# The end of a hybrid trunk step rebuilt: the last expert's activations, down products and scatters

## The reference

```python
h2 = rms_norm(x, g_ffn) * (1.0 + sc_f) + sh_f
# for each expert e and each of its tokens:
hu = xe @ w_up[e] + b_up[e]
gate = jnp.minimum(hu[:, :D_FF], 7.0)
lin = jnp.clip(hu[:, D_FF:], -7.0, 7.0)
y = ((lin + 1.0) * gate * sigmoid(1.702 * gate)) @ w_down[e] + b_down[e]
# out[token] = sum over its 4 experts of softmax weight * y
x = x + gt_f * out
y_prompt, y_sample = rms_norm(x_prompt, g_final), rms_norm(x_sample, g_final)
```

## Time and profile before

| what | value |
|---|---|
| median of 3 runs | 1298.41 us (1296.67 to 1298.94) |
| the profiled execution's own time | 1295.37 us |
| its span, first to last instruction | 1293.6 us |
| TensorE matmul busy | 1163.6 us (90%) |
| TensorE weight loads busy | 567.3 us (44%) |
| DVE, ACT, POOL busy | 375.8, 182.7, 72.0 us |
| moved by DMA | 467.36 MB, mean 361 GB/s |
| mean granted TensorE clock | 0.970 of full speed |

### The profile page before, as it was taken

One profiled execution on the slowest core, in us unless ns is written; L12 is line 12 of the kernel. 1 busy time (PEld: TensorE's weight loads), 2 busy tenths in 40 slices (PEclk: granted clock), 3 DMA queues, 4 the chain that ended last, 5 costly groups with the idle time before them and its releaser, 6 DMA issues.

```text
span 1293.6 us, 23349 instructions
## 1 busy us (share of the span) xinstructions
PE 1163.6 (90%) x8690; PEld 567.3 (44%) x8691; DVE 375.8 (29%) x819; ACT 182.7 (14%) x358; POOL 72.0 (6%) x178
## 2 busy tenths in 40 slices
PE   5999999996989999998999998999777889988986
PEld 4655447544335446443344544444223334343332
DVE  0164214848211222321222121142211221222235
ACT  3112232213010111110110110010100000110101
POOL 1010001431000000000000000000000000000001
PEclk9999999998899999998999999999879999989999
DMA  9944635883689999999999999999999999999992
GB/s 366 363 152 172 239 131 196 253 317 138 260 351 424 409 417 427 427 428 425 428 424 426 426 426 428 426 376 428 427 426 428 426 425 426 426 426 428 427 422 85
DMA packets 62481, 467.36 MB, mean 361 GB/s; under 512 B 6538, under 2 KB 24910, under 8 KB 26730
## 3 DMA queue, kind: packets, MB, share of 16 engines
q1 hardware_dynamic: 59770, 461.86, 86.7%
q10 hardware_dynamic: 2288, 4.37, 1.1%
q0 software_dynamic: 384, 0.59, 0.2%
HBM read 459.78 MB, written 6.42 MB: 360 GB/s over the span
## 4 chain that ended last, share of the span: by engine, by line
PE 58%; DMA 36%; DVE 2%; issue 2%; ACT 1%; POOL 0%; SPq 0%; ACTq 0%; POOLq 0%; DVEq 0%
DMA mem<-in_w_up 33%; PE psum L1048 20%; PE psum L1096 9%; PE psum L680 6%; PE psum L1106 5%; PE psum L661 3%; PE psum L1008 3%; PE psum L867 2%; PE psum L684 2%; DMA mem<-in_in_chunks 1%; PE psum L536 1%; DMA mem<-in_mod_chunks 1%; PE psum L1058 1%; PE psum L871 1%; PE psum L1052 1%
## 5 line engine op out<-in xcount | busy, mean ns | idle before, releaser
L1048 PE MATMUL psum<-mem 128*32 128x512 f32 (+2 forms) x2432 | 399.9, 628 | 74.0 <-DMA mem<-in_w_up 66.8
L1048 PEld LDWEIGHTS psum<-mem 128*32 128x32 f32 (+2 forms) x2432 | 133.7, 123 | 330.3 <-issue 203.4
L1096 PE MATMUL psum<-mem 128*32 128x512 f32 (+3 forms) x1024 | 207.8, 594 | 0.0
L2172 DVE TENSOR_SCALAR mem<-psum 128x256 f32<-128x256 f32 (+3 forms) x32 | 19.2, 601 | 542.6 <-PE psum L1052 542.6
L1106 PE MATMUL psum<-mem 128*128 128x512 f32 x360 | 143.1, 608 | 3.3 <-DVE mem L2173 2.2
L1096 PEld LDWEIGHTS psum<-mem 128*32 128x32 f32 (+3 forms) x1024 | 93.3, 127 | 87.4 <-issue 61.2
L2205 DVE TENSOR_TENSOR mem<-mem,psum 128x1024 f32<-128x1024 f32 (+1 forms) x90 | 94.1, 1045 | 95.8 <-PE psum L1106 95.8
L680 PE MATMUL psum<-mem 128*128 128x512 f32 x192 | 84.2, 595 | 0.0
L1008 PEld LDWEIGHTS psum<-mem 128*128 128x128 bf16 x2232 | 74.7, 99 | 19.4 <-issue 19.1
L1496 ACT ACTIVATE mem<-mem 128x256 f32<-128x256 f32 (+3 forms) x32 | 17.9, 561 | 451.0 <-DVE mem L2172 451.0
L1008 PE MATMUL psum<-mem 128*128 128x64 bf16 (+1 forms) x2232 | 78.4, 196 | 0.0
(11 more groups left out here) (279 smaller groups left out, 803.4 us busy)
## 6 DMA issues: line engine op xcount, KB each, us to landing
mem<-in_w_up SPq DMA_DIRECT2D x128, 2048.0 KB, 22.3
mem<-in_w_down SPq DMA_DIRECT2D x128, 1024.0 KB, 15.9
mem<-in_mod_chunks SPq DMA_DIRECT2D x12, 2048.0 KB, 12.3
mem<-in_in_chunks SPq DMA_DIRECT2D x8, 2048.0 KB, 9.9
mem<-in_out_chunks SPq DMA_DIRECT2D x2, 2048.0 KB, 10.0
mem<-in_x_prompt ACTq DMA_DIRECT2D x2, 1024.0 KB, 6.9
mem<-in_state_ret SPq DMA_DIRECT2D x4, 512.0 KB, 8.7
mem<-in_state_mlstm_c SPq DMA_DIRECT2D x4, 512.0 KB, 7.7
```

What stands on the lines that cost most here:

```text
L1048: last = pe.matmul(out, xg[:, 2 * c + h, cols], moving, start=(c + h == 0), stop=False)
L1096: last[c] = pe.matmul(psum[slots * q:slots * q + slots, 6 + u, :], turned, place(c, 2, D)[:, piece % 2, 512 * u:512 * u + 512], start=(j = ...
```

## The change

The last expert's turned activations get a buffer of their own (`actT_last`), so ACT copies them without the wait for expert 30's down products; that wait (`down_before`) now stands ahead of the copy into `yd` alone. The last expert's down products go to banks 4 and 5 in place of 6 and 7, without the wait for `y_copied` ahead of them and without the scatter in their middle. Both scatters, expert 30's and expert 31's, stand behind them: samples of 30, prompt tile 0 of 30, samples of 31, prompt tile 0 of 31, prompt tile 1 of 30, prompt tile 1 of 31; prompt tile 1 uses banks 6 and 7. ACT's round for expert 31 is taken out of its loop and written out (`expert_usual_end`), with a no-operation in place of the copy of gathered tokens. The load of g_final is issued behind the copy of the last routing weights. DVE adds prompt tile 0, waits for g_final, scales the samples, adds prompt tile 1, and scales both prompt tiles. Where an expert has more than 128 tokens another path runs, which keeps `actT`. Lines that only pass a buffer on are left out.

```diff
--- before.py
+++ after.py
@@ -220,6 +220,7 @@
         yd_last = at(2 * SLOT, 2, 512); G_last = at(2 * SLOT + D, NTOK)
+        actT_last = at(2 * SLOT + 2 * D, KD, 128)
@@ -1060,9 +1061,9 @@
-            def down(it, slots, meanwhile=None):
-
-                end = meanwhile is not None
+            def down(it, slots, end=False, acts=actT):
+
+                first = 4 if end else 6
@@ -1073,27 +1074,25 @@
                 for u in range(2):
-                    pe.matmul(psum[0:slots, 6 + u, :], bsel_down[:, 0:slots],
+                    pe.matmul(psum[0:slots, first + u, :], bsel_down[:, 0:slots],
                               bparts[:, 2 * D + 512 * u:2 * D + 512 * u + 512], start=True, stop=False)
                 last = [None] * DOWN
                 for j in range(pieces):
-                    if end and j == pieces // 2:
-                        meanwhile()
                     for u in range(2):
...
                             else:
-                                turned = actT[:, j, slots * q:slots * q + slots]
+                                turned = acts[:, j, slots * q:slots * q + slots]
...
-                            last[c] = pe.matmul(psum[slots * q:slots * q + slots, 6 + u, :], turned,
+                            last[c] = pe.matmul(psum[slots * q:slots * q + slots, first + u, :], turned,
@@ -1163,35 +1162,38 @@
-            def last_expert(its, count):
+            def last_expert(its, count, acts):
 
                 pe.wait_ge(S("G_ready"), its + 1)
                 pe.wait_ge(S("added"), 3 * its + CLEARED)
                 turn_weights(its, 1)
-
-                def scatter_before():
-
-                    pe.wait_ge(S("G_ready"), its + 1)
-                    pe.wait_ge(S("y_copied"), its + 1)
+                by_size(pe, count, lambda slots: down(its - 1, slots, True, acts))
+                pe.wait_ge(S("G_ready"), its + 1)
+                pe.wait_ge(S("y_copied"), its + 1)
+
+                def samples(weights, rows, first):
                     for u in range(2):
-                        pe.matmul(psum[64 * u:64 * u + 64, 0, :], G[:, tok(2)], yd[:, u, :], start=True, stop=False)
-                    pe.wait_ge(S("y_gated"), 2)
-                    for t in range(2):
-                        for u in range(2):
-                            pe.matmul(psum[:, 2 + 2 * t + u, :], G[:, tok(t)], yd_gated[:, u, :], start=True, stop=False)
-
-                pe.wait_ge(S("y_copied"), its + 1)
-                by_size(pe, count, lambda slots: down(its - 1, slots, scatter_before))
+                        if not first:
+                            pe.wait_ge(S("y_copied"), its + 2 + u)
+                        last = pe.matmul(psum[64 * u:64 * u + 64, 0, :], weights[:, tok(2)], rows[:, u, :],
+                                         start=first, stop=not first)
+                    return last
+
+                def prompt(t, weights, rows, first):
+                    for u in range(2):
+                        last = pe.matmul(psum[:, (2, 6)[t] + u, :], weights[:, tok(t)], rows[:, u, :],
+                                         start=first, stop=not first)
+                    return last
+
+                samples(G, yd, True)
+                pe.wait_ge(S("y_gated"), 2)
+                prompt(0, G, yd_gated, True)
                 pe.wait_ge(S("G_ready"), its + 2)
-                for u in range(2):
-                    pe.wait_ge(S("y_copied"), its + 2 + u)
-                    last = pe.matmul(psum[64 * u:64 * u + 64, 0, :], G_last[:, tok(2)], yd_last[:, u, :], start=False, stop=True)
-                last.then_inc(S("last_scattered"), 1)
+                samples(G_last, yd_last, False).then_inc(S("last_scattered"), 1)
                 pe.wait_ge(S("y_gated"), 4)
-                for t in range(2):
-                    for u in range(2):
-                        last = pe.matmul(psum[:, 2 + 2 * t + u, :], G_last[:, tok(t)], yd_last_gated[:, u, :], start=False, stop=True)
-                    last.then_inc(S("last_scattered"), 1)
+                prompt(0, G_last, yd_last_gated, False).then_inc(S("last_scattered"), 1)
+                prompt(1, G, yd_gated, True)
+                prompt(1, G_last, yd_last_gated, False).then_inc(S("last_scattered"), 1)
@@ -1496,21 +1498,20 @@
-            def copy_turned(it, slots, down_before):
+            def copy_turned(it, slots, dst, behind_down=False):
                 n = 8 * slots
                 src = flat(4, n)
                 act.wait_ge(S("act_turned"), it + 1)
-                if down_before:
-                    for c in range(DOWN):
-                        act.wait_ge(piece_done[UP + c], it)
+                if behind_down:
+                    down_before(it)
...
-                act.copy(actT.rearrange("p j s -> p (j s)")[:, 0:n], src).then_inc(S("actT_ready"), 1)
+                act.copy(dst.rearrange("p j s -> p (j s)")[:, 0:n], src).then_inc(S("actT_ready"), 1)
@@ -1526,20 +1527,35 @@
+            def down_before(it):
+
+                for c in range(DOWN):
+                    act.wait_ge(piece_done[UP + c], it)
+
+            def expert_usual_end(count):
+
+                by_size(act, count, lambda slots: sigmoid(NE - 1, slots))
+                act.wait_ge(S("gathered"), NE + 1)
+                act.nop().then_inc(S("xg_ready"), 1)
+                copy_weights(NE - 1)
+                by_size(act, count, lambda slots: copy_turned(NE - 1, slots, actT_last))
+                down_before(NE - 1)
                 act.copy(yd.rearrange("p u n -> p (u n)"), flat(6, D)).then_inc(S("y_copied"), 1)
 
             def last_expert(its):
 
                 act.wait_ge(S("Pg_turned"), its + 1)
                 act.copy(G_last, psum[:, 1, 0:NTOK]).then_inc(S("G_ready"), 1)
+                act.dma_start(gfin.rearrange("p u n -> p (u n)"), a["g_final"].partition_broadcast(128))\
+                    .then_inc(S("gfin_in"), 16)
                 for c in range(DOWN):
                     act.wait_ge(piece_done[c], its + 1)
-                act.copy(yd_last[:, 0, :], psum[:, 6, :]).then_inc(S("y_copied"), 1)
+                act.copy(yd_last[:, 0, :], psum[:, 4, :]).then_inc(S("y_copied"), 1)
                 act.wait_ge(S("y_gated"), 3)
-                act.copy(yd_last[:, 1, :], psum[:, 7, :]).then_inc(S("y_copied"), 1)
-                act.dma_start(gfin.rearrange("p u n -> p (u n)"), a["g_final"].partition_broadcast(128))\
-                    .then_inc(S("gfin_in"), 16)
+                act.copy(yd_last[:, 1, :], psum[:, 5, :]).then_inc(S("y_copied"), 1)
@@ -1560,14 +1576,16 @@
-            with act.Fori(1, NE) as e:
+            with act.Fori(1, NE - 1) as e:
                 expert(0, e, e, count_at(e + 1), count_at(e + 2))
             most = act.value_load(counts_i[0:1, NE + 2:NE + 3], min_val=0, max_val=NTOK)
             with act.If(most <= BIG_BLOCK):
+                expert_usual_end(count_at(NE))
                 last_expert(NE)
             with act.Else():
+                expert(0, NE - 1, NE - 1, count_at(NE), count_at(NE + 1))
@@ -2221,7 +2239,7 @@
-                TT(yd_last_gated[:, 1, :], psum[:, 7, :], gateF_p[:, 512:D], ALU.mult).then_inc(S("y_gated"), 1)
+                TT(yd_last_gated[:, 1, :], psum[:, 5, :], gateF_p[:, 512:D], ALU.mult).then_inc(S("y_gated"), 1)
@@ -2230,15 +2248,24 @@
-                for t in range(2):
+
+                def add_last(t):
                     dve.wait_ge(S("last_scattered"), 2 + t)
-                    TT(x2[:, t, :], x2[:, t, :], flat(2 + 2 * t, D), ALU.add).then_inc(S("x3_ready"), 1)
-                dve.wait_ge(S("gfin_in"), 16)
-                for i, t in enumerate(LAST_ORDER):
+                    TT(x2[:, t, :], x2[:, t, :], flat((2, 6)[t], D), ALU.add).then_inc(S("x3_ready"), 1)
+
+                def scale(i):
+                    t = LAST_ORDER[i]
                     n = ROWS[t]
                     dve.wait_ge(S("rstd3"), i + 1)
                     STT(x2[0:n, t, :], x2[0:n, t, :], rs[0:n, t:t + 1], gfin.rearrange("p u n -> p (u n)")[0:n, :],
                         ALU.mult, ALU.mult).then_inc(S("y_final"), 1)
+
+                add_last(0)
+                dve.wait_ge(S("gfin_in"), 16)
+                scale(0)
+                add_last(1)
+                scale(1)
+                scale(2)
```

More of the change, by code:

```diff
@@ L1086, in down @@
                             if slots == 96:
-                                turned = actT.rearrange("p j s -> p (j s)")[:, 0:8 * slots] \
+                                turned = acts.rearrange("p j s -> p (j s)")[:, 0:8 * slots] \
                                     .rearrange("p (j s) -> p j s", j=KD)[:, piece, :]
                             else:
-                                turned = actT[:, j, slots * q:slots * q + slots]
+                                turned = acts[:, j, slots * q:slots * q + slots]
                             if last[c] is None:
@@ L1214, in _ @@
             with pe.If(most <= BIG_BLOCK):
```

(20 more changed lines are left out.)

## The result

In the first comparison the changed kernel took 1289.07 us (median of 4 runs, 1288.86 to 1290.37) against 1298.55 before: a ratio of 0.9945, interval 0.9923 to 0.9967. The forecast, 1293.9 with a range of 1292.3 to 1296.4, had the direction and half the size. Two later comparisons with more runs gave 0.9950 (0.9932 to 0.9968; 12 runs against 35) and 0.9969 (0.9955 to 0.9983; again 12 against 35), that is 6.4 and 3.9 us between the means. In both of these, 12 more runs of the kernel before were taken beside them; counted in, the means lie 6.2 and 4.5 us apart. So there are two questions: what the change gives, and why the comparisons differ.

A forecast was written before the change was run, and what follows sets the result against it. The prediction took the loop as DMA-bound until 1244.25, then a chain through TensorE, DVE, ACT and POOL. The last scaling moves from 1290.32 to 1285.76, 4.56 us less, so 1298.41 becomes 1293.85 (forecast 1293.9, range 1292.3 to 1296.4).

The forecast's parts named there:

- The waits: TensorE idle ahead of expert 31's down products (ACT's copy into yd) and behind them (ACT's copies, DVE's gating); 1265.29 and 1277.45.
- own buffer and own banks: Start of expert 31's down products: without the wait for yd at 1264.12 in place of 1265.29, 1.17 us earlier.
- Down products and scatters: Expert 31's down products in one piece, 7.46 us; scatters follow, samples ending at 1275.12 and tile 1 at 1280.58.
- The cover: Behind the last down products, expert 30's samples and prompt tile 0 (2.68 us) hide DVE's 1.71 us, 0.97 to spare.
- The tail: DVE, ACT and POOL behind the samples' scatter: the last scaling ends at 1285.76, before 1290.32.
- The wait of tile 1's addition behind the scaling of the samples: On DVE at the end: tile 1, scattered at 1280.58, is added 0.6 us late, until 1282.36.
- POOL's 0.19 us: POOL's L1598 for tile 1 at the end: taken as 0.18 us; at 1.10 the end would come 0.92 later.
- The edits at nothing: ACT's written-out round, shorter loop, omitted copy and moved g_final load cost nothing; bound: a 1.28 us table load shows.
- the base of 1298.41: Median time of the kernel before, from three runs; less 4.56 us it gives 1293.85.
- Theory B: From the follow-ups: something the change moves also shortens the loop, so what lies ahead of the end takes 3 to 4 us less.
- Late instructions: Rival: jumps into and out of the last down products stall TensorE, one 2.31 us (0.10), both 3.58 each (0.03).
- The tail gave nothing back: Rival at the kernel's end: POOL's long time leaves 3.64 us of gain, a table load 3.28; chance 0.13.

The follow-up runs named there:

- the filled kernel: The kernel before with 8 and 4 unused products keeping TensorE busy at its two waits of the end; 0.9997 and 1.0011 of before.

## Why the prediction was wrong in size

**The waits.** Right in kind: both are gone, nothing took their place. The entry "own buffer and own banks" was mis-sized. The forecast took 0.81 us between two weight loads as the price of the branches and started the products 1.17 us earlier; counted from the last up products they start 1.92 us earlier (20.99 us behind them before, 1262.01 - 1242.94 = 19.07 after). A gap between weight loads is no gap between products: the changed trace has the same 0.81 ahead of line 1184, with no branch there, while TensorE's products follow one another without a pause. The 0.75 us between the copy's end and the products in the earlier trace rows belong to the wait and went with it; the run with the wait back, 1.40 us longer, had 0.76 again. That they are the price of the branches behind a wait is an argument from the chain of before, where a wait without branches, ahead of the samples' scatter, cost 0.14:

```profile
1277.85 0.59 ACT mem L1538
1278.44 0.14 issue
1278.58 1.48 PE psum L1188 x4
```

These rows also show that TensorE had work again from 1278.58, behind ACT's first copy, and not from 1279.16, behind the last gating, as the forecast reads it; its sum does not use that.

**Down products and scatters.** From the products' start to the samples' last scatter: 11.00 us forecast, 1273.31 - 1262.01 = 11.30 measured; the scatters came to 0.86, 1.92 and 1.03 where the forecast had 0.86, 1.82 and 0.86. The cover held.

**The tail.** From the samples to the last scaling 10.61 us forecast, 10.67 measured. The wait of tile 1's addition behind the scaling of the samples came as told, and so did POOL's 0.19 us. The store took 0.18 less. So the end: 4.56 + 0.75 - 0.30 - 0.06 + 0.18, about 5.1 us, against 5.14 measured.

**The edits at nothing.** The forecast put nothing for the loop, since "no edit touches the loop's loads". Yet the last load of w_up ends 0.4 us later in the traces of the changed loop, as told above; a small term, but one against the gain.

**The step that failed most: taking one trace and three runs for the kernel.** Two terms of the sum rest on it.

The first is the gain. The forecast said of the windows that the granted clock is 1.00 and had no term for it. In two of four traces of before it fell behind the very wait that the change removes, at 1.7 us each; in none of the seven traces of the changed kernel and its kin without that wait. If one execution in two falls, that is some 0.9 us more on average, an estimate from four traces which the times of the filled kernel did not confirm. The end's 5.1, the load's -0.4 and this 0.9 make 5.6 us where the forecast had 4.56, and the two later comparisons measured 6.2 and 4.5.

The second is the base of 1298.41 and the width of the range. The three runs of before spanned 2.3 us, and the range was widened by half of that (by its own terms that gives 1292.4 to 1296.2; 1292.3 to 1296.4 is written). In the later comparisons the runs of before lay between 1290.2 and 1302.2; the mean of all 114 is 1296.6, so the base was 1.8 us high. The changed kernel's medians were 1289.07, 1290.01 and 1291.78, below the range in all three comparisons; a base of 1296.6 less 5.6 gives 1291.0, which lies among them.

This scatter arises ahead of the stretch: its start lies between 1243.6 and 1248.4 in the six traces with before's loop, and between 1240.4 and 1250.4 in the twelve with the changed one, with means of 1245.9 and 1244.8. It is there before the last eleven loads of w_up in the chain, which together take 324.7 to 325.6 us in every trace: the load ahead of them ends between 914.8 and 925.4. What makes it stays open. Theory B is not borne out, since the one thing that the change was seen to move there costs time; but the two means are uncertain by about 1 us each, so a shift of 1 to 2 us is not ruled out. The first comparison's 9.5 us hold the end's 5 to 6; the other 3 to 4 no run explains. With the scatter of the later runs, the difference between two means of four is uncertain by about 1.7 us, and this is twice that. I take it for chance; that is not shown.

**The rivals.** Late instructions did not come: 0.07 us into the down products, and no pause out of them. The Trainium skill's rule on jumps ("Runtime: NRT & Kernel Launch", section "Instruction fetch mechanics") asks for no stop here if the code lies within the window, which no run here shows. One packet of another instruction queue, q8, passed at 1262.1, just behind the first of these products, and they went on. The tail gave nothing back: no table load showed, and ACT idled 16.79 us ahead of the last sigmoid in its written-out round, as in the earlier trace rows.

## What to carry to other kernels

Where an engine waits just before a long run of products, count the wait, the branches behind it, and the clock that it may cost afterwards; a trace without a fall does not show that the kernel has none. A gap between two weight loads is not a price for the products: look at the products themselves. Put independent products behind the long run rather than into its middle, so that they cover the copies of its result. And before a range is set, ask how far runs scatter: three runs within 2.3 us came from a kernel that spans 12.

## What was not expected of the hardware

An idle time of 1.8 to 1.9 us ahead of the products was followed by half clock in two traces of four, one of 3.4 us in two of two, one of 1.4 in none of one, and the first two filled with needless products in none of four. The loss, 1.7 us and 3.15, was not much less than the idle time that led to it. That filling costs nothing where it fits into the wait was seen in the stretch alone, not in the times.
